# Attention on one TensorE queue: the filler matmuls stand ahead of a group of scores

## The reference

```python
q = rms_norm((h @ w_q).reshape(b, s, N_HEADS, 2, HEAD_DIM), q_norm)      # 8 heads, 2 maps, 64 wide
for i in range(s // Q_BLOCK):                                            # 4 blocks of 128 queries
    sc = einsum('bqhcd,bkhcd->bhcqk', qb, kb) * scale                    # keys 0 .. (i+1)*128
    p = softmax(where(causal, sc, NEG_INF))
    a = p[:, :, 0] - lam * p[:, :, 1]
    outs.append(einsum('bhqk,bkhe->bqhe', a, vb))
o = rms_norm(concatenate(outs), sub_norm) * (1.0 - lam_init)
x = x + o.reshape(b, s, N_HEADS * V_DIM) @ w_o
```

## Time and profile before

| | |
|---|---|
| Time, median of 3 runs | 1101.98 us (1101.8 to 1102.21) |
| The profiled execution's own time | 1102.19 us |
| Its span in the trace | 1100.4 us |
| PE busy in the span | 1092.2 us (99%) |
| DVE, ACT busy | 782.6 us (71%), 479.9 us (44%) |
| PE's granted clock | 1.00 in every slice |

### The profile page before, as it was taken

One profiled execution on the slowest core, in us unless ns is written; L12 is line 12 of the kernel. 1 busy time (PEld: TensorE's weight loads), 2 busy tenths in 40 slices (PEclk: granted clock), 3 DMA queues, 4 the chain that ended last, 5 costly groups with the idle time before them and its releaser, 6 DMA issues.

```text
span 1100.4 us, 13443 instructions
## 1 busy us (share of the span) xinstructions
PE 1092.2 (99%) x5168; PEld 901.1 (82%) x5168; DVE 782.6 (71%) x980; ACT 479.9 (44%) x695; POOL 77.3 (7%) x58
## 2 busy tenths in 40 slices
PE   8999999999999999999999999999999999999998
PEld 7888888888888888888888877788888888888887
DVE  4765554787787787788764488965678688678686
ACT  7221234354354353354632367855444344344342
POOL 0000012000000000001430032103000000000000
PEclk9999999999999999999999999999999999999999
DMA  7433463314414315301333201045314414314202
GB/s 192 99 94 101 133 212 96 104 50 154 114 40 159 109 38 172 96 1 39 96 115 96 95 21 39 2 157 150 96 58 134 116 58 145 104 58 152 78 1 77
DMA packets 144752, 105.90 MB, mean 96 GB/s; under 512 B 12592, under 2 KB 121136, under 8 KB 144688
## 3 DMA queue, kind: packets, MB, share of 16 engines
q1 hardware_dynamic: 143648, 105.03, 31.4%
q10 hardware_dynamic: 1040, 0.00, 0.1%
HBM read 102.93 MB, written 2.10 MB: 95 GB/s over the span
## 4 chain that ended last, share of the span: by engine, by line
PE 98%; DMA 1%; ACT 0%; DVE 0%; issue 0%; SPq 0%; ACTq 0%; DVEq 0%
PE ps L603 32%; PE ps L630 28%; PE ps L490 20%; PE ps L692 10%; PE ps L717 2%; PE ps L756 2%; PE ps L779 2%; PE ps L768 1%; DMA kv<-in_x 1%; PE ps L759 1%; PE ps L572 0%; PE ps L666 0%; PE ps L585 0%; PE ps L737 0%; PE ps L791 0%
## 5 line engine op out<-in xcount | busy, mean ns | idle before, releaser
L603 PE MATMUL ps<-h,w_hi 128*128 128x512 f32 x1024 | 316.2, 390 | 0.0
L630 PE MATMUL ps<-w_hi,h 128*128 128x512 f32 x896 | 277.4, 389 | 0.0
L603 PEld LDWEIGHTS ps<-h,w_hi 128*128 128x128 f32 x1024 | 191.5, 188 | 39.4
L603 PE MATMUL ps<-h,w_lo 128*128 128x512 f32 x512 | 199.3, 389 | 0.0
L630 PEld LDWEIGHTS ps<-w_hi,h 128*128 128x128 f32 x896 | 168.2, 188 | 34.9
L490 PE MATMUL ps<-h,w_hi 128*128 128x512 f32 x608 | 187.9, 390 | 0.0
L630 PE MATMUL ps<-w_lo,h 128*128 128x512 f32 x448 | 174.3, 389 | 0.0
L969 ACT ACTIVATE w_hi<-b_raw 128x1024 fp32r<-128x1024 f32 x80 | 82.0, 1054 | 141.5 <-PE ps L603 81.9
L490 PEld LDWEIGHTS ps<-h,w_hi 128*128 128x128 f32 x608 | 113.6, 188 | 23.4 <-DVE w_lo L1243 0.2
L490 PE MATMUL ps<-h,w_lo 128*128 128x512 f32 x304 | 118.3, 389 | 0.0
L1305 DVE TENSOR_TENSOR w_lo<-b_raw,w_hi 128x1024 fp32r<-128x1024 f32 x80 | 95.9, 1223 | 26.4 <-ACT w_hi L969 26.4
(11 more groups left out here) (136 smaller groups left out, 1203.0 us busy)
## 6 DMA issues: line engine op xcount, KB each, us to landing
b_raw<-in_w_down SPq DMA_DIRECT2D x64, 512.0 KB, 4.5
w_raw<-in_w_up SPq DMA_DIRECT2D x64, 512.0 KB, 4.0
w_raw<-in_a_w_in SPq DMA_DIRECT2D x23, 512.0 KB, 3.7
w_raw<-in_w_kv SPq DMA_DIRECT2D x16, 512.0 KB, 3.7
w_raw<-in_a_w_out SPq DMA_DIRECT2D x8, 512.0 KB, 4.0
w_raw<-in_w_q SPq DMA_DIRECT2D x8, 512.0 KB, 3.5
w_raw<-in_w_o SPq DMA_DIRECT2D x8, 512.0 KB, 4.1
kv<-in_x SPq DMA_DIRECT2D x4, 512.0 KB, 6.7
```

The lines of the kernel that those rows point to most:

```text
L603: last = nc.tensor.matmul(ps[:, v % 4, :], w[:, s_, k * P:(k + 1) * P], h_of[inp][:, half, k, :], start=(k == 0 and i == 0), stop=(k == KC ...
L630: last = nc.tensor.matmul(ps[:, CHAIN[p][tb], :], op[half][:, k, tb * P:(tb + 1) * P], w[:, s_, cols], start=(FRESH[p] and k == 0 and i == ...
```

## The change

In heads 0 to 2, the projection's first two parts go from behind `scores(n+2)` and `scores(n+3)` to ahead of them, and its third part from ahead of `weights_T(n+2)` to behind it, ahead of `scores(n+5)`. In heads 3 to 7 the output projection's chunk goes from behind `scores(n+3)` to ahead of it, with the wait for `s_qsq` in head 3, and head 3's second chunk from behind `values(n+1)` to ahead of `scores(n+4)`. No instruction is added, removed or resized; the other engines' programs are the same.

```diff
             for h in range(H):
                 n = 4 * h
-                scores(n + 2)
                 if h < 3:
                     project(5 + h, range(0, 3))
+                scores(n + 2)
                 weights_T(n)
                 if n:
                     values(n - 1)
 
-                scores(n + 3)
                 if h < 3:
                     project(5 + h, range(3, 6))
                 if h == 3:
                     pe.wait_ge(s_qsq, 16)
                 if h >= 3:
                     project_out(0, WO_FILL[h, 1])
+                scores(n + 3)
                 weights_T(n + 1)
 
+                if h == 3:
+                    project_out(0, WO_FILL[h, 2])
                 if h < H - 1:
                     scores(n + 4)
                 values(n)
                 values(n + 1)
-                if h == 3:
-                    project_out(0, WO_FILL[h, 2])
                 if h == H - 1:
                     pe.wait_ge(s_exp, 2 * STEPS - 2)
                     project_out(1, range(0, 3))
                 if h < 4:
                     queries_T(4 + h)
+                weights_T(n + 2)
+
                 if h < 3:
                     project(5 + h, range(6, KC))
-                weights_T(n + 2)
-
                 if h < H - 1:
                     scores(n + 5)
```

## The result

| | before | after |
|---|---|---|
| Time, median | 1102.02 us (1101.8 to 1102.51, 22 runs) | 1103.61 us (1103.3 to 1104.12, 22 runs) |
| Ratio after to before | | 1.0014, 95% interval 1.0008 to 1.002 |
| Span of the profiled execution | 1100.4 us | 1102.3 us |

The change costs 1.6 us of 1102. The forecast was +1.7 us, 1103.7 us. The interval of the ratio lies above 1, so the kernel is slower in truth, by 0.14%.

The account below looks back on a forecast made before the run. PE, busy 99%, was taken to bound the kernel, with a PE-DVE ring in heads 4 to 6. Terms 1.6 + 0.3 - 0.2 + 0 + 0 gave +1.7 us, 1103.7 us; 8 in 10: 1101.7 to 1105.5.

Parts of the forecast that it names:

- Heads 4 to 6: The chunk delays scores(n+3), row_max(n+3), join(n+2), so PE waits at weights_T(n+2): 0.53 us a head, +1.6 us.
- the forecast's 1.22: Time in us from the start of 512-wide scores to their row_max, used to place row_max(23) at 704.09.
- Heads 0 to 2: Larger projection parts moved: a gain of 0.5 us once against 0.8 us of new waits, sum +0.3 us.
- Head 0's covered wait: The first part ahead of scores(2) fills PE's 0.45 us wait for q_lo(2): -0.5 us, once.
- The new wait behind the second part: In heads 0 to 2, PE waits 0.28 us a head for DVE ahead of weights_T(n+2): +0.8 us.
- The sign that the prediction named for it: In heads 0 to 2, PE idle of about 0.3 us ahead of weights_T(n+2).
- Head 3: The existing wait at weights_T(12) partly takes up PE's lateness from earlier heads: -0.2 us.
- Head 7 and the switches: Head 7's chunk ahead of scores(31), and fifteen groups of scores now following a filler: nothing for either.
- switch: Rival: scores behind a filler cost 0.10 us extra at fifteen places, +1.5 on top, 1105.2 us; chance 0.12.
- hidden: Rival: row_max(n+3) has slack, so DVE's lateness does not show; 1101.7 us, chance 0.10.
- all heads: Rival: heads 0 to 3 also lose 0.5 us each, minus head 0's gain; 1105.0 us, chance 0.13.
- The granted clock: Rival: PE's clock falls to 1.2 GHz in the attention's waits, 1112 us; chance 0.01.

Follow-up runs that it names:

- e3: The changed kernel with join(n+2) of heads 4 to 6 over 128 of its 384 columns, so its output differs; 1103.59 us, ratio 1.0013.
- f1: The kernel before with only head 0's first projection part (nine matmuls) moved ahead of scores(2); 1101.50 us, ratio 0.9995.
- f3: The kernel before with, in heads 0 to 2, the second projection part ahead of scores(n+3) and the third behind weights_T(n+2); 1102.60 us, ratio 1.0005.
- e2: The changed kernel with the chunks of heads 4 to 7 put back behind scores(n+3); 1102.01 us, ratio 0.9998 to before.
- e4: The kernel before with the chunks of heads 4 to 6 moved behind weights_T(n+1), directly ahead of scores(n+4); 1102.06 us, ratio 0.9999.
- e1: The kernel before with only the chunks of heads 4 to 6 moved ahead of scores(n+3); 1103.72 us, ratio 1.0013.
- b2: The kernel before with three filler moves (head 0, heads 0 to 2, head 7), plus scores(n+6) ahead of values(n+2) in heads 3 to 6; 1104.17 us.

## Why the prediction was right

**Heads 4 to 6, +1.6 us, measured +1.65 in the change and +1.60 alone.** The step named the place, the wait and its size: `row_max(23)` at 704.09 against its real 704.92 - 0.83 = 704.09 (head 5 begins 0.83 us later in the changed kernel than before; the forecast's 1.22 is 1.05 + 0.18 and should be 1.23, on which nothing hangs); the chunk to scores in 0.88 against 0.87 (702.82 to 703.69); a head of 9.0 us against 9.05. The wait was forecast at 0.7 us from start to start. In the changed kernel `values(21)` start at 705.72, and where no wait follows, as in head 1 of the same kernel, it takes 0.72 us from values to the next transposes (662.40 to 663.12). So `weights_T(22)` could have started at 706.44 and started at 707.18, 0.74 us late; the 0.58 of the trace counts from the modelled end of the values. Not all of this wait is new: by the same count it was 0.15 us before (704.93 + 0.72 to 705.80), which only the weight loads of the kernel before show:

```profile
705.80 0.31 PEld L768 LDWEIGHTS ps<-ident,kv 128*128 128x128 f32 x3 [0.18 <-DVE kv L1592]
```

**One branch of two.** The prediction said that PE waits for the join. It does, but e3 shows that a faster join would not have helped: `scores(n+5)` wait for the exponentials until the same moment. The sum held because both branches start at `row_max(n+3)`, so that the lateness enters ahead of both. The prediction did not have the second branch, so here the number came out right without the whole path being known. The branch was in reach in the trace of before, and no row of the prediction shows it: ACT's last instruction of `exps(23)` ends at 706.25, PE's `scores(25)` start at 706.30:

```profile
706.05 0.20 ACT L1112 ACTIVATION_READ_ACCUMULATOR kv<-ps,nmax 128x1 f32 x1
```

```profile
706.30 0.61 PE L756 MATMUL ps<-ah,h 64*128 64x256 f32 x6
```

**Heads 0 to 2.** Head 0's covered wait: forecast -0.5, measured -0.54 (f1). The new wait behind the second part: forecast 0.28 a head, 0.31 in f3, and 0.25 in the change, by the starts of `scores(5)`, `scores(9)` and `scores(13)` (from `scores(0)`: 13.22, 26.36 and 39.86 us before, 12.95, 26.34 and 40.08 after). Sum forecast +0.3, measured +0.22. The sign that the prediction named for it, idle time of PE ahead of `weights_T(n+2)`, is seen in the weight loads and not in PE's own row.

**Head 3.** Forecast -0.2, measured -0.36 after a start 0.22 later. The step's reason was wrong: it had the chain hang on the last part of the projection, "which ends about when it did". Before, the chain hung on `evacuate(10)`, in front on ACT. In the change it hangs on the last part, which ends later, but `take_q(7)` still starts 0.17 us earlier (40.19 us after `scores(0)` against 40.36). Those 0.17 and the 0.22 that heads 0 to 2 had lost are what head 3 gives back, within 0.03. This is the term with the largest error, 0.16 us.

**Head 7 and the switches.** Nothing was forecast for either, and nothing was measured (4.43 us in both; e2 and e4). The 0.10 us between a filler and scores is there, and it is paid ahead of any group of scores.

The whole against the single runs: 1.7 forecast, 1.59 by the medians, 1.51 by the traces. The rivals fell to e2 and e4 (switch), e1 (hidden) and e2 (all heads: heads 0 to 3 together cost nothing). The granted clock stayed at 1.00 in heads 4 and 5, through the new waits of 0.58 us.

## What to carry to other kernels

When two engines in order hand work to each other, follow the ring once round and ask of each moved instruction which result it makes later, and what stands behind that result's consumer. Here three matmuls ahead of `scores(n+3)` cost 0.55 us a head, because `row_max(n+3)` stands ahead of `join(n+2)`; behind these scores they cost nothing, on either side of `weights_T(n+1)`. A filler belongs where the trace shows a wait. Before you test such a rule, check that the experiment really makes the other result late; e4 did not. Look for a second branch of equal length before you shorten one, and before you move work ask what it was covering where it stood: b2 lost 3.6 us for that.

## What the runs showed of the hardware

From the end of a DVE or ACT instruction to the start of the PE matmuls that wait for it the traces show 0.05 us: in the changed kernel `join(22)` ends at 707.13 and its transposes start at 707.18; in e3 the exponentials end at 706.96 and the scores start at 707.01.

Ahead of each group of 64-row matmuls PE's timeline has a gap of about 0.1 us, behind transposes and behind fillers alike: two transposes to scores take 0.31 us and four 0.53, which is 0.11 for each and 0.09 more, and a 512-column matmul of a filler to scores takes 0.33 where one of its own kind follows after 0.23. Behind values the difference is larger, 0.99 us to scores against 0.81 to a filler; how much of that belongs to the scores is open.

A short wait can be missing from PE's waits, as the modelled ends of the matmuls in front cover it in part or in full; the weight loads show it, as the 0.38 us in head 1 of the changed kernel.

Executions of nearly the same program reached the same instruction, `scores(0)`, from 638.62 to 639.40 us of their spans, which is as much as half of what this change moved: differences below 1 us were read from a common instruction, not from the start of the span.
